# Gather depth, order of diagonals and evictions, and place of a residual in a PEER layer behind two transformer blocks

## The chip, the cores and the metric

The kernel runs on one core of one Trainium2 chip. The metric is the device time of one execution in microseconds, the median of several runs. Engines are named as in the profile: PE is TensorE (PEld its weight loads), DVE is VectorE, ACT is ScalarE, POOL is GpSimd and SP is SyncE.

## The reference

256 tokens of width 1024 pass through a first block (two layers, each with two SwiGLU FFNs around an attention mixer) and a second block, which ends with a PEER layer. Only that last layer is touched here. In outline, for a block of 128 tokens `xb` (normalized), with 8 heads, 128 sub-keys and a top 16:

```
q = (xb @ w_q).reshape(128, 8, 2, 128)
scores = einsum('thpd,hpkd->thpk', q, sub_keys)
top_s, top_i = top_k(scores, 16)
cand = all 16*16 sums of the two halves' scores
best_s, best_pos = top_k(cand, 16)
expert = index of the best (one of 16384)
gate = softmax(best_s)
act = gelu(einsum('thkd,td->thk', u[expert], xb))
y = einsum('thk,thkd->td', gate * act, v[expert])
```

`x + y` is the output. Everything is float32. Each token reads 8 x 16 = 128 experts, and an expert is a row of `u` and a row of `v`, 1024 numbers each.

## The kernel before, in words

Everything ahead of the PEER layer is a stream of weight units: SP loads a unit into one of nine `raw` tiles, ACT and DVE split it into a high and a low part, and TensorE multiplies. The change doesn't touch that part.

The PEER layer has two interwoven halves.

**Units.** The query projection `pq` has 16 units n, each 128 columns of `w_q` (16 matmuls on plain weights, L2044; the first five units are split ones). ACT evicts the unit's result into `QP` (L929). Two units make a head: after units 1, 4, 6, 8, 10, 12, 14 and 15 (`scored(n)`) TensorE computes that head's scores (L2061), and ACT evicts them (L935). Before unit n starts, TensorE waits for the eviction of unit n-1 or of the scores before it, since units and scores share two PSUM banks. DVE chooses the experts of a head in six steps (`route`, L1426 to L1469), which gives 16 index columns for each block of tokens. `shares` subtracts the maximum on DVE (L1477), ACT takes the exp (L904), and `gates` on DVE divides (L1482 to L1486).

**Slots.** The 2 x 128 pairs (block of tokens, expert rank) are 256 slots g. For slot g:

- POOL gathers 128 rows of `u` and `v` side by side into a tile of 128 x 2048 (L622, 1 MB). It waits until gather g-`FLYING` has landed, and until the slot that used the tile before is done on TensorE (`s_y`), or, for a tile's first use, until its former content is.
- DVE multiplies the `u` half with the tokens and sums (L1509, "dot").
- ACT applies gelu (L912), scales by the gate (L916), and writes a diagonal matrix of the weights (L920), into one of four buffers, so it waits for slot g-4 on TensorE.
- TensorE multiplies the diagonal with the `v` half (L2023, two matmuls of 512 columns) and adds into two PSUM banks of the block (`YB`). The residual enters the same banks at first, by eight matmuls with the identity (`begin`, L2013).

There are 15 tiles. Ten are free when the first gathers go; `raw` tiles are added when the last unit that used them is done: one at gather 10 (units 7 and 8), one at gather 14 (unit 10), one at gather 22 (unit 12), one at gather 34 (unit 15), and with it `XF`, the last unit's input.

**The order.** The order on each engine is written out. On TensorE and ACT, units 9 to 15 are mixed with slots 0 to 27: behind unit n come slots 4(n-9) to 4(n-9)+3 (`mixed(n)`); then slots 28 to 255 follow alone. On ACT the eviction of unit n comes ahead of these four slots' diagonals. DVE does the choosing of later heads ahead of every second slot: the table `CHOOSING` gives step number i of the list `later` to slot 2i, where twelve `route` steps, `shares` and `gates` of a pair of heads make 14 entries. ACT does the exp of `shares` ahead of the same slot in its own order. The first pair of heads is outside the table: its exp comes on ACT behind unit 8. The first residual, `begin(0)`, stands behind unit 8 on TensorE; the second, `begin(1)`, whose banks the units use until unit 15, behind slot 27.

```
for n in range(16):
    ac.wait_ge(*queried(n))
    ...
    if n == 8:
        shares(0, 0, 2)
    for g in mixed(n):
        slot(g)
```

Of the kernel before, what the change touches and what calls it, by code (L numbers as in the profile page):

```python
# [234 lines left out]
SLOTS = 15  # L235
QN_RING = 6
MIX0, MIX = 9, 4
FLYING = 4
ARENA = 17024


# [15 lines left out]
def program(nc, wst, cst, x, skt, uv, out, vscr, units):  # L257
    ctx = ExitStack()
    with ctx:
# [3 lines left out]
        def sem(name):  # L263
            return ctx.enter_context(nc.semaphore(name))
# [34 lines left out]
        def c(name, lo=0, hi=None):  # L299
            a0, a1 = at[name]  # L300
            return C[:, a0 + lo:(a1 if hi is None else a0 + hi)]

        def f32(ap):
            return ap.bitcast(F32)

        def flat(ap):
            return ap.rearrange("p a b -> p (a b)")
# [122 lines left out]
        s_txf, s_xtt, s_qp, s_scm, s_scr = (sem(n) for n in ("x_gained", "x_turned", "pq_out", "pq_scores",  # L430
                                                                 "scores_out"))
# [14 lines left out]
        def U(name, n):  # L446

            return split[where[name][n]] + 1
# [29 lines left out]
        def queried(n):  # L478

            if where["pq"][n] in split:  # L480
                return s_used, U("pq", n)
            return s_plain, plain_n[where["pq"][n]]
# [4 lines left out]
        def scored(n):  # L487
            return (0,) if n == 1 else (n // 2 - 1,) if n % 2 == 0 and n >= 4 else (7,) if n == 15 else ()

        def mixed(n):  # L490
            return range(MIX * (n - MIX0), MIX * (n - MIX0 + 1)) if n >= MIX0 else ()
# [10 lines left out]
        for k in sorted(range(4), key=lambda k: max(last[2 * k], last[2 * k + 1])):  # L502
            n = max(last[2 * k], last[2 * k + 1])
# [5 lines left out]
        for g in range(256):  # L509
            n = min((n for n in range(SLOTS) if rows[n][2] <= g), key=lambda n: taken[n][-1] if taken[n] else -1)  # L510
# [12 lines left out]
        CHOOSING, GATES = {}, {(0, 0): 1}  # L523
# [5 lines left out]
                    later += [("route", blk, hh, k) for hh in (h, h + 1) for k in range(6)]  # L529
                    later += [("shares", blk, h, 2), ("gates", blk, h, 2)]  # L530
        for n, what in enumerate(later):
            CHOOSING[2 * n] = (what,)

        def three(pe, o, wh, wl, xh, xl, start, stop):
            pe.matmul(o, wh, xh, start=start, stop=False, skip_group_check=True)  # L535
# [34 lines left out]
        def pool_program(po):  # L570
# [40 lines left out]
            for g in range(256):  # L611
                blk, s = g // 128, g % 128
                row, free, _ = rows[home[g]]
                if s % 16 == 0:
                    po.wait_ge(s_exi, g // 16 + 1)
                if g >= FLYING:
                    po.wait_ge(s_g[home[g - FLYING]], 16 * turn_of[g - FLYING])
                if before[g] is None:
# [7 lines left out]
        def act_program(ac):  # L626
# [3 lines left out]
            def hi(name, n):  # L630

                while at_m[0] < min(U(name, n) + AHEAD - 1, NSPL):
                    m = at_m[0]
                    i = spl_unit[m]
                    w = units[i][1]
                    ac.wait_ge(s_raw[i % RAW], 16 * (i // RAW + 1))
                    if m >= SPL:
                        ac.wait_ge(s_used, m - SPL + 1)
                    ac.activation(WH[:, m % SPL, 0:w], raw[:, i % RAW, 0:w], ACT.Copy).then_inc(s_hi, 1)  # L639
                    at_m[0] = m + 1  # L640
# [27 lines left out]
            def root(p):  # L668
                ac.wait_ge(s_sums, p + 1)
                ac.activation(RT[:, 0, :], PS[:, 7, 0:T], ACT.Sqrt, bias=c("eps", 0, 1), scale=1.0 / D).then_inc(s_rt, 1)  # L670
# [76 lines left out]
            for t in range(2):  # L747
                hi("uk", t)
                ac.wait_ge(s_pad, 1)
                for e in range(4):  # L750
                    n = 4 * t + e
# [93 lines left out]
            n = 4  # L845
# [54 lines left out]
            def shares(blk, h0, n):  # L900

                ac.wait_ge(s_bd, GATES[blk, h0])
                bd = BD[:, h0:h0 + n, :]
                ac.activation(bd, bd, ACT.Exp, scale=RTK[:, blk:blk + 1]).then_inc(s_bde, 1)  # L904

            def slot(g):
                blk, s = g // 128, g % 128
                for what in CHOOSING.get(g, ()):
                    if what[0] == "shares":
                        shares(*what[1:])  # L910
                ac.wait_ge(s_dot, g + 1)
                own(ac.activation(AG[:, blk, s:s + 1], AV[:, blk, s:s + 1], ACT.Gelu, scale=RTK[:, blk:blk + 1]))  # L912
                own.wait()
                if s % 32 == 0:
                    ac.wait_ge(s_gate, g // 32 + 1)
                own(ac.activation(WV[:, blk, s:s + 1], AG[:, blk, s:s + 1], ACT.Copy, scale=GA[:, blk, s:s + 1]))  # L916
                own.wait()
                if g >= 4:
                    ac.wait_ge(s_y, g - 3)
                ac.activation(DG[:, g % 4, :], c("ident"), ACT.Copy, scale=WV[:, blk, s:s + 1]).then_inc(s_dg, 1)  # L920
                if g == 127:
                    ac.wait_ge(s_y, 128)
                    ac.activation(OT[0], flat(PS[:, YB[0]:YB[0] + 2, :]), ACT.Copy).then_inc(s_ot, 1)

            for n in range(16):
                ac.wait_ge(*queried(n))
                if n >= QN_RING:
                    ac.wait_ge(s_scm, (n - QN_RING) // 2 + 1)
                ac.activation(QP[:, n % QN_RING, :], PS[:, bank_q[n], 0:T], ACT.Copy).then_inc(s_qp, 1)  # L929
                if n == 0:  # L930
                    hi("pq", 1)
                for h in scored(n):
                    ac.wait_ge(s_scm, h + 1)
                    for blk in range(2):
                        ac.activation(flat(SC[blk][:, 2 * h:2 * h + 2, :]), PS[:, bank_s[h], 256 * blk:256 * blk + 256],  # L935
                                      ACT.Copy).then_inc(s_scr, 1)
                if n == 1:
                    for kc in range(8):
                        ins = ac.activation(XF[:, kc, :], hT[:, kc, :], ACT.Copy, scale=c("gains", 64 + kc, 65 + kc))
                    ins.then_inc(s_txf, 1)  # L940
                    root(7)
                if n == 8:
                    shares(0, 0, 2)
                for g in mixed(n):
                    slot(g)

            for g in range(MIXED, 256):
# [569 lines left out]
        def pe_program(pe):  # L1517
# [195 lines left out]
            for n in range(8):  # L1713
                kv, g = n // 4, n % 4
# [37 lines left out]
            for r in range(4):  # L1752
                for t in range(2):
                    g = 2 * t + r % 2
# [26 lines left out]
            for e in range(2):  # L1781
                for blk in range(2):
                    for j in range(8):
                        g = 2 * (j // 4) + e
# [225 lines left out]
            def begin(blk):  # L2010

                for kc in range(8):
                    pe.matmul(PS[:, YB[blk] + kc // 4, 128 * (kc % 4):128 * (kc % 4) + 128],  # L2013
                              hT[:, kc, 128 * blk:128 * blk + 128], c("ident"), start=kc % 4 == 0, stop=False,
                              skip_group_check=True)

            def slot(g):
                blk, s = g // 128, g % 128
                pe.wait_ge(s_g[home[g]], 16 * turn_of[g])
                pe.wait_ge(s_dg, g + 1)  # L2020
                v = f32(rows[home[g]][0][:, 1024:2048])
                for q in range(2):
                    ins = pe.matmul(PS[:, YB[blk] + q, :], DG[:, g % 4, :], v[:, 512 * q:512 * q + 512], start=False,  # L2023
                                    stop=s == 127, skip_group_check=True)
                    if g == 255 and q == 0:
                        ins.then_inc(s_left, 1)
                ins.then_inc(s_y, 1)

            for n in range(16):
# [42 lines left out]
                    begin(0)  # L2072
                for g in mixed(n):
                    slot(g)
            pe.wait_ge(s_scr, 16)
            begin(1)
            for g in range(MIXED, 256):
                slot(g)

        block = ctx.enter_context(nc.Block())  # L2080
# [9 lines left out]
        @block.scalar  # L2090
        def _(eng):
            act_program(eng)
# [5 lines left out]
        @block.tensor  # L2098
        def _(eng):
            pe_program(eng)  # L2100
# [29 lines left out]
```

## Time and profile before

| | |
|---|---|
| median of 3 runs | 2061.48 us (2056.69 to 2062.80) |
| the profiled execution, its own time | 2058.03 us |
| its span | 2056.2 us |
| mean granted clock of TensorE | 0.969 |
| busy: PE, DVE, ACT, POOL | 1861.9, 1302.4, 907.1, 305.5 us |
| moved by DMA | 488.36 MB, of it 274.74 MB on the queue of POOL's gathers |

The span is what the profiler covers; the execution's own time is a little longer. Rows of the timelines stand in microseconds from the span's start. The PEER layer's first gather is issued at 1379.13 us, and the last dot begins at 2048.60 us. A busy share above 1 for the DMA engines means that packets overlap.

### The profile page before, as it was taken

Reading aid. Unit: us, or ns where it says so; the run is one execution under the profiler, and the core shown is the slowest. Engines: PE = TensorE matmul, PEld = TensorE weight load, DVE = VectorE, ACT = ScalarE, POOL = GpSimd, SP = SyncE. Lnnn points to the kernel's source line nnn. Section 1 sums busy time; section 2 is a strip of 40 time slices with the busy share of each in tenths; the row PEclk is TensorE's granted clock in tenths of the full one; section 3 lists DMA queues with packets and bytes.
Section 4 is the critical chain, followed back from the end, with each engine's and each line's share of the span. In section 5 each row is a group of like instructions: output and inputs, shape, how many; then the busy total and the mean of one; then the engine's idle time right before and its main releaser. Section 6 shows DMA issues by size and latency. Waiting matters only on the chain.

```text
span 2056.2 us, 29871 instructions
## 1 busy us (share of the span) xinstructions
PE 1861.9 (91%) x11568; PEld 1494.0 (73%) x11568; DVE 1302.4 (63%) x2378; ACT 907.1 (44%) x1865; POOL 305.5 (15%) x340
## 2 busy tenths in 40 slices
PE   7999999999999999999999988898897887777777
PEld 7999889999999999769999878786442332222222
DVE  5555885555655562786556766578297777776444
ACT  4444464444444431474444443543354444444333
POOL 1000101000100010000000000122333333333332
PEclk9999999999999997999999899999999999999999
DMA  7555426955455534205555233359899999999998
GB/s 272 185 185 177 132 72 145 315 186 185 154 185 185 185 123 145 82 27 171 184 187 182 87 129 103 114 184 367 316 418 421 421 421 418 419 420 417 414 422 346
DMA packets 96973, 488.36 MB, mean 238 GB/s; under 512 B 10640, under 2 KB 10896, under 8 KB 63808
## 3 DMA queue, kind: packets, MB, share of 16 engines
q0 software_dynamic: 38368, 274.74, 34.8%
q1 hardware_dynamic: 58464, 211.70, 30.2%
q8 instruction: 93, 1.52, 0.3%
q14 instruction: 48, 0.39, 0.1%
HBM read 482.21 MB, written 4.19 MB: 237 GB/s over the span
## 4 chain that ended last, share of the span: by engine, by line
PE 64%; issue 10%; DVE 10%; DMA 8%; POOL 5%; ACT 4%; POOLq 0%; ACTq 0%; SPq 0%; DVEq 0%
PE PS L535 16%; PE PS L537 15%; PE PS L536 15%; PE PS L2023 6%; DMA raw<-uv,A 2%; PE PS L2044 2%; DVE WL L967 2%; PE PS L1538 1%; DMA XL<-uv,A 1%; POOL raw L622 1%; DVE XL L975 1%; DMA A<-uv,A 1%; DMA XF<-uv,A 1%; DVE A L1267 1%; POOL WH L622 1%
## 5 line engine op out<-in xcount | busy, mean ns | idle before, releaser
L967 DVE TENSOR_TENSOR WL<-raw,WH 128x1024 fp32r<-128x1024 f32 (+1 forms) x379 | 451.6, 1233 | 92.3 <-ACT WH L639 91.7
L535 PE MATMUL PS<-XH,WH 128*128 128x256 f32 x1632 | 473.5, 290 | 30.0 <-DVE WL L967 16.0
L536 PE MATMUL PS<-XL,WH 128*128 128x256 f32 x1632 | 465.7, 285 | 0.0
L537 PE MATMUL PS<-XH,WL 128*128 128x256 f32 x1632 | 465.6, 285 | 0.0
L639 ACT ACTIVATE WH<-raw 128x1024 fp32r<-128x1024 f32 (+1 forms) x379 | 375.0, 1040 | 65.5 <-PE PS L537 34.2
L535 PEld LDWEIGHTS PS<-XH,WH 128*128 128x128 f32 x1632 | 315.0, 193 | 39.0 <-issue 19.4
L536 PEld LDWEIGHTS PS<-XL,WH 128*128 128x128 f32 x1632 | 315.6, 193 | 0.2
L537 PEld LDWEIGHTS PS<-XH,WL 128*128 128x128 f32 x1632 | 315.1, 193 | 0.0
L912 ACT ACTIVATE A<-A,RTK 128x1 f32<-128x1 f32 x256 | 74.9, 293 | 289.9 <-DVE A L1509 288.4
L535 PE MATMUL PS<-GH,WH 128*128 128x256 f32 x704 | 198.1, 281 | 0.0
L536 PE MATMUL PS<-GL,WH 128*128 128x256 f32 x704 | 197.8, 281 | 0.0
L537 PE MATMUL PS<-GH,WL 128*128 128x256 f32 x704 | 197.8, 281 | 0.0
L680 ACT ACTIVATE A<-A 128x256 f32<-128x256 f32 x88 | 36.7, 417 | 351.0 <-DVE A L996 351.0
L580 POOL TENSOR_TENSOR A<-hT 128x256 f32<-128x256 f32 x64 | 47.0, 756 | 953.1 <-DVE hT L1011 726.1
L535 PE MATMUL PS<-YH,WH 128*128 128x256 f32 x584 | 166.3, 285 | 5.2 <-DVE A L1115 3.1
L536 PE MATMUL PS<-YL,WH 128*128 128x256 f32 x584 | 165.1, 283 | 0.0
L537 PE MATMUL PS<-YH,WL 128*128 128x256 f32 x584 | 165.0, 283 | 0.0
L2023 PE MATMUL PS<-raw,A 128*128 128x512 f32 x260 | 127.7, 617 | 31.5 <-ACT A L920 31.5
L996 DVE TENSOR_TENSOR A<-PS,RT 128x512 f32<-128x512 f32 x88 | 60.8, 691 | 149.8 <-PE PS L537 149.4
L535 PEld LDWEIGHTS PS<-GH,WH 128*128 128x128 f32 x704 | 132.7, 188 | 0.1
L537 PEld LDWEIGHTS PS<-GH,WL 128*128 128x128 f32 x704 | 132.7, 188 | 0.0
L536 PEld LDWEIGHTS PS<-GL,WH 128*128 128x128 f32 x704 | 132.7, 188 | 0.0
(305 smaller groups left out, 3128.2 us busy)
## 6 DMA issues: line engine op xcount, KB each, us to landing
raw<-wst SPq DMA_DIRECT2D x388, 512.0 KB, 4.5
raw<-wst SPq DMA_DIRECT2D x9, 384.0 KB, 3.6
vscr<-A POOLq DMA_DIRECT2D x1, 3072.0 KB, 36.0
A<-vscr POOLq DMA_DIRECT2D x1, 2048.0 KB, 21.9
C<-cst SPq DMA_DIRECT2D x1, 1236.5 KB, 11.0
raw<-uv,A POOLq DMA_INDIRECT x65, 9.7
hT<-xin SPq DMA_DIRECT2D x2, 512.0 KB, 5.3
A<-vscr POOLq DMA_DIRECT2D x1, 1024.0 KB, 11.8
```

What stands on the lines that cost most here:

```text
L535: pe.matmul(o, wh, xh, start=start, stop=False, skip_group_check=True)
L536: pe.matmul(o, wh, xl, start=False, stop=False, skip_group_check=True)
L537: return pe.matmul(o, wl, xh, start=False, stop=stop, skip_group_check=True)
L580: po.tensor_tensor(SQ[:, kc, :], hT[:, kc, :], hT[:, kc, :], ALU.mult).then_inc(s_sq, 1)
L622: po.indirect_dma_start(row, None, uv if row.dtype == F32 else uv.bitcast(F32R), bass.IndirectOffsetOnAxis(ap=EX[:, blk, s:s + 1].bitcast( ...
L639: ac.activation(WH[:, m % SPL, 0:w], raw[:, i % RAW, 0:w], ACT.Copy).then_inc(s_hi, 1)
L680: ac.activation(GS[:, b, 0, :], GS[:, b, 0, :], ACT.Silu).then_inc(s_silu, 1)
L912: own(ac.activation(AG[:, blk, s:s + 1], AV[:, blk, s:s + 1], ACT.Gelu, scale=RTK[:, blk:blk + 1]))
L967: dv.tensor_tensor(WL[:, m % SPL, 0:w], raw[:, i % RAW, 0:w], f32(WH[:, m % SPL, 0:w]), ALU.subtract).then_inc(s_lo, 1)
L996: dv.tensor_tensor(GS[:, b], PS[:, b, :].rearrange("p (a t) -> p a t", a=2), RT[:, 1:2, :].broadcast_to([128, 2, T]), ALU.mult).then_inc(s ...
L2023: ins = pe.matmul(PS[:, YB[blk] + q, :], DG[:, g % 4, :], v[:, 512 * q:512 * q + 512], start=False, stop=s == 127, skip_group_check=True)
L2044: ins = pe.matmul(PS[:, bank_q[n], 0:T], R[:, 128 * kc:128 * kc + 128], XF[:, kc, :], start=kc == 0, stop=kc == 7, skip_group_check=True)
```

## The change

It has five edits. POOL lets up to eight gathers fly (`FLYING` 4 to 8). ACT makes the diagonals of the first two slots of `mixed(n)` ahead of the eviction of unit n, and the other two behind it. The exp of the first pair of heads stands behind unit 6 on ACT. The table `CHOOSING` starts at slot 2, so each of its steps comes two slots later, on DVE and for the exps on ACT. TensorE adds the second residual ahead of slot 64. Lines behind L925 are numbered two higher in the changed kernel, and those of TensorE's slots, too.

```diff
--- before.py
+++ after.py
@@ -235,7 +235,7 @@
 SLOTS = 15
 QN_RING = 6
 MIX0, MIX = 9, 4
-FLYING = 4
+FLYING = 8
 ARENA = 17024
 
 
@@ -529,7 +529,7 @@
                     later += [("route", blk, hh, k) for hh in (h, h + 1) for k in range(6)]
                     later += [("shares", blk, h, 2), ("gates", blk, h, 2)]
         for n, what in enumerate(later):
-            CHOOSING[2 * n] = (what,)
+            CHOOSING[2 * n + 2] = (what,)
 
         def three(pe, o, wh, wl, xh, xl, start, stop):
             pe.matmul(o, wh, xh, start=start, stop=False, skip_group_check=True)
@@ -923,6 +923,8 @@
                     ac.activation(OT[0], flat(PS[:, YB[0]:YB[0] + 2, :]), ACT.Copy).then_inc(s_ot, 1)
 
             for n in range(16):
+                for g in mixed(n)[:2]:
+                    slot(g)
                 ac.wait_ge(*queried(n))
                 if n >= QN_RING:
                     ac.wait_ge(s_scm, (n - QN_RING) // 2 + 1)
@@ -939,9 +941,9 @@
                         ins = ac.activation(XF[:, kc, :], hT[:, kc, :], ACT.Copy, scale=c("gains", 64 + kc, 65 + kc))
                     ins.then_inc(s_txf, 1)
                     root(7)
-                if n == 8:
+                if n == 6:
                     shares(0, 0, 2)
-                for g in mixed(n):
+                for g in mixed(n)[2:]:
                     slot(g)
 
             for g in range(MIXED, 256):
@@ -2072,9 +2074,10 @@
                     begin(0)
                 for g in mixed(n):
                     slot(g)
-            pe.wait_ge(s_scr, 16)
-            begin(1)
             for g in range(MIXED, 256):
+                if g == 64:
+                    pe.wait_ge(s_scr, 16)
+                    begin(1)
                 slot(g)
 
         block = ctx.enter_context(nc.Block())
```

On ACT, around unit 10 (L929, L931 in the changed kernel, evicts the unit; L935 or L937 its scores; L912, L916 and L920 are one slot), the order was:

```order
L929 ACTIVATE A<-PS 128x256
L935 ACTIVATE A<-PS 128x256 x2
L912 ACTIVATE A<-A,RTK 128x1
L916 ACTIVATE A<-A 128x1
L920 ACTIVATE A<-C,A 128x128
L912 ACTIVATE A<-A,RTK 128x1
L916 ACTIVATE A<-A 128x1
L920 ACTIVATE A<-C,A 128x128
```

and is now:

```order
L912 ACTIVATE A<-A,RTK 128x1
L916 ACTIVATE A<-A 128x1
L920 ACTIVATE A<-C,A 128x128
L912 ACTIVATE A<-A,RTK 128x1
L916 ACTIVATE A<-A 128x1
L920 ACTIVATE A<-C,A 128x128
L931 ACTIVATE A<-PS 128x256
L937 ACTIVATE A<-PS 128x256 x2
```

Slots 4 and 5 have moved from behind the two evictions to ahead of them.

On ACT, from unit 5 to unit 9, with the exp of the first pair of heads (L904) and the loads of the tables for exp and gelu, the order was:

```order
L929 ACTIVATE A<-PS 128x256 x2
L935 ACTIVATE A<-PS 128x256 x2
L929 ACTIVATE A<-PS 128x256 x2
L935 ACTIVATE A<-PS 128x256 x2
L904 ACT_TABLE_LOAD
L904 ACTIVATE A<-A,RTK 128x32
L929 ACTIVATE A<-PS 128x256
L912 ACT_TABLE_LOAD
```

and is now:

```order
L931 ACTIVATE A<-PS 128x256 x2
L937 ACTIVATE A<-PS 128x256 x2
L904 ACT_TABLE_LOAD
L904 ACTIVATE A<-A,RTK 128x32
L931 ACTIVATE A<-PS 128x256 x2
L937 ACTIVATE A<-PS 128x256 x2
L912 ACT_TABLE_LOAD
L912 ACTIVATE A<-A,RTK 128x1
```

The exp has moved ahead of the evictions of units 7 and 8; the gelu table's load now stands right behind unit 8's scores, where unit 9's eviction stood before it.

On ACT, around unit 15, with the exp of the second pair of heads (L904), the order was:

```order
L929 ACTIVATE A<-PS 128x256
L935 ACTIVATE A<-PS 128x256 x2
L904 ACT_TABLE_LOAD
L904 ACTIVATE A<-A,RTK 128x32
L912 ACT_TABLE_LOAD
L912 ACTIVATE A<-A,RTK 128x1
L916 ACTIVATE A<-A 128x1
L920 ACTIVATE A<-C,A 128x128
```

and is now:

```order
L912 ACTIVATE A<-A,RTK 128x1
L916 ACTIVATE A<-A 128x1
L920 ACTIVATE A<-C,A 128x128
L912 ACTIVATE A<-A,RTK 128x1
L916 ACTIVATE A<-A 128x1
L920 ACTIVATE A<-C,A 128x128
L931 ACTIVATE A<-PS 128x256
L937 ACTIVATE A<-PS 128x256 x2
L904 ACT_TABLE_LOAD
L904 ACTIVATE A<-A,RTK 128x32
L912 ACT_TABLE_LOAD
L912 ACTIVATE A<-A,RTK 128x1
```

Slots 24 and 25 stand ahead of the last eviction, and the second exp still stands between that eviction and the next diagonal, which is now slot 26's.

## Rows read from the trace of the kernel before

**Rows 1.** The page, part 2: GB/s in 40 equal slices of 51.4 us
```profile
GB/s 272 185 185 177 132 72 145 315 186 185 154 185 185 185 123 145 82 27 171 184 187 182 87 129 103 114 184 367 316 418 421 421 421 418 419 420 417 414 422 346
```

**Rows 2.** Windows: stretch, its us, busy us of each engine (x instructions), PEclk, DMA share, GB/s
```profile
1380.00:1408.00 28.00, 25.23 (x148) 22.52 (x146) 14.87 (x62) 8.13 (x19) 9.59 (x11) 0.99 1.02 395
1408.00:1500.00 92.00, 78.16 (x238) 44.74 (x239) 52.50 (x139) 34.95 (x109) 28.32 (x30) 0.93 0.88 330
1500.00:2040.00 540.00, 432.18 (x910) 160.74 (x909) 364.01 (x879) 235.03 (x680) 202.17 (x215) 0.98 1.05 420
```

**Rows 3.** Waits, 1404 to 1503 us: who waited <- for whom: sum, times, longest
```profile
ACT A L929 <- PE PS L2044: 52.7, 7, 10.2
...
POOL raw L622 <- PE PS L2044: 17.9, 3, 7.7
```

**Rows 4.** Timeline of POOL: start, us, instruction [idle before <- releaser]
```profile
1412.67 0.94 POOL L622 DMA_INDIRECT XH<-uv,A  x1 [7.87 <-PE PS L2023]
...
1439.13 1.10 POOL L622 DMA_INDIRECT WL<-uv,A  x1 [5.98 <-PE PS L2023]
...
1486.28 0.94 POOL L622 DMA_INDIRECT raw<-uv,A  x1 [7.69 <-PE PS L2044]
...
1500.94 0.94 POOL L622 DMA_INDIRECT A<-uv,A  x1 [1.58 <-DMA raw<-uv,A]
...
2038.91 0.94 POOL L622 DMA_INDIRECT YL<-uv,A  x1 [1.54 <-DMA A<-uv,A]
```

**Rows 5.** Timeline of TensorE, 1400 to 1505 us
```profile
1408.16 3.75 PE L2023 MATMUL PS<-XH,A 128*128 128x512 f32 x4 [2.93 <-ACT A L920]
...
1446.81 1.05 PE L2061 MATMUL PS<-A 128*128 128x128 f32 x8
1449.64 1.96 PE L2023 MATMUL PS<-XL,A 128*128 128x512 f32 x4 [1.78 <-ACT A L920]
...
1491.97 3.75 PE L2023 MATMUL PS<-XH,A 128*128 128x512 f32 x4 [4.84 <-ACT A L920]
...
1500.92 1.95 PE L2013 MATMUL PS<-C,hT 128*128 128x128 f32 x16
```

**Rows 6.** Timeline of ACT, 1398 to 1495 us
```profile
1401.99 0.32 ACT L904 ACTIVATE A<-A,RTK 128x32 f32<-128x32 f32 x1
...
1405.67 1.28 ACT L912 ACT_TABLE_LOAD   x1
...
1485.53 0.38 ACT L929 ACTIVATE A<-PS 128x256 f32<-128x256 f32 x1 [7.90 <-PE PS L2044]
1487.17 0.66 ACT L935 ACTIVATE A<-PS 128x256 f32<-128x256 f32 x2 [1.25 <-PE PS L2061]
...
1491.42 0.40 ACT L920 ACTIVATE A<-C,A 128x128 f32<-128x128 f32 x1
```

**Rows 7.** Timeline of DVE, 1390 to 1492 us
```profile
1394.00 0.18 DVE L1477 TENSOR_TENSOR A<-A 128x32 f32<-128x32 f32 x1
...
1445.84 1.22 DVE L1509 CUSTOM_DVE_ANT_0 WL<-WL,PS 128x1024 fp32r<-128x1024 f32 x1 [1.54 <-DMA WL<-uv,A]
...
1461.76 1.22 DVE L1509 CUSTOM_DVE_ANT_0 XL<-XL,PS 128x1024 fp32r<-128x1024 f32 x1 [1.26 <-DMA XL<-uv,A]
...
1489.49 0.19 DVE L1482 TENSOR_REDUCE A<-A 128x2 f32<-128x32 f32 x1 [26.50 <-ACT A L904]
```

**Rows 8.** The chain that ended last, merged: start, us, what
```profile
1443.52 3.45 PE PS L2044 x16
...
1502.87 37.78 PE PS L2023 x88
```

**Rows 9.** Windows of 4 and 5 us, the same columns
```profile
1400.00:1404.00 4.00, 4.00 (x28) 3.72 (x28) 1.55 (x9) 2.26 (x4) 1.07 (x2) 1.00 1.07 430
1408.00:1412.00 4.00, 3.84 (x5) 1.80 (x6) 3.90 (x12) 2.88 (x10) 0.00 (x0) 0.50 0.92 375
15.00:20.00 5.00, 5.00 (x33) 5.00 (x32) 3.78 (x4) 2.34 (x2) 0.00 (x0) 1.00 1.03 410
```

## The prediction

> **What bounds the kernel now.** I read the page's slices first: the last quarter moves 420 GB/s in slice after slice, while the first slices of the PEER part reach 316 to 418 [rows 1]. The windows put numbers on it. From 1500 to 2040 us the core moves 420 GB/s with DMA engines booked over 100%; from 1408 to 1500 it moves only 330; before that 395 [rows 2]. Each of the 256 gathers is 128 rows x 2048 x 4 bytes, 1.049 MB, and at 420 GB/s takes 2.50 us. So the tail is bound by the DMA engines, and time can be won in two ways only: by keeping them busy between 1408 and 1500, or by making them faster. The first stretch moved 92 x 330 = 30.4 MB, worth 72.3 us at 420, so **19.7 us are lost there, and that is the ceiling** of anything that only reorders work (some 1.7 us more in the 28 us at 395).
>
> Who loses them: the waits of 1404 to 1503 show POOL held 17.9 us by TensorE's weight units (L2044), and ACT 52.7 us at its eviction (L929), waiting for the same units [rows 3]. POOL's timeline shows it at single gathers: 11 leaves at 1412.67 after 7.87 us of waiting for a slot, 34 at 1486.28 after 7.69 us for a unit, 41 at 1500.94; from there to gather 255 at 2038.91 it is 214 gathers at 2.514 us [rows 4]. TensorE and ACT take turns: ACT evicts unit n, only then makes the diagonals of its four slots, and TensorE idles meanwhile: 2.93 us before slot 0, 1.78 us in a middle unit, 4.84 us before slot 24 [rows 5]. ACT's rows show what stands in that last gap: the eviction at 1485.53, the scores at 1487.17, and slot 24's diagonal only at 1491.42 [rows 6]. In between stand two table loads and the exp of the second gates, for which DVE waited 26.50 us, to 1489.49 [rows 7].
>
> **The parts of the change.**
>
> *Two diagonals ahead of each eviction.* Needed for it are dots 4k and 4k+1 (k = 0 to 6) before unit 9+k ends. DVE had dot 25 done at 1463.0, 22 us before unit 15's eviction [rows 6, 7], so the input is there. ACT then makes both diagonals while TensorE is in the slots and the unit before, and TensorE finds them when its unit ends. Its chain from the end of unit 9 (1408.16 - 2.93 = 1405.2 [rows 5]) to slot 28 becomes: 28 slots at 37.78/22 = 1.72 us, 48.1; six units at 3.45, 20.7; four score groups at 1.05 less their overlap with the next matmul, 0.9, in sum 3.6 [rows 5, 8]; the wait of unit 15's scores for its own eviction, 0.6. Unit 15 still has an exp between its eviction and slot 26. From that eviction's start to the end of the first diagonal behind the exp ACT took 1485.53 to 1491.82, 6.3 us [rows 6]; TensorE covers it with scores and slots 24 and 25, 5 us, which leaves a stall of 1.3. The sum is 74.3: slot 28 starts at 1479.5. Before, that point was 1502.87 [rows 8]. **TensorE's chain becomes 23.4 us shorter**, of which idle time is 14.8 (2.93, five gaps of about 1.66, 4.84, less the 1.3), the second residual 1.8, and most of the rest slow stretches: the granted clock was 0.50 at 1408 to 1412 [rows 9], the 1.2 GHz level, after 2.93 us of idling, and slot 0's matmuls took 3.75 us where slot 12's took 1.96, behind a gap of 1.78 us only [rows 5].
>
> *What the gathers make of it.* Gather g takes the tile that slot g-11 used (11 to 13), later g-12 (15 to 21), g-13 (23 to 33) and g-15; gathers 14, 22 and 34 wait for units 10, 12 and 15 instead. With an idle pipe a gather needs 1445.84 - 1439.13 = 6.7 us from its issue on POOL to the start of its dot [rows 4, 7], and two are at least 2.50 apart. Gather 10 is through at about 1413 (the engines run to nearly 1412 [rows 9]). By the chain above slots 0 to 3 end at 1407.0, 1408.7, 1410.4 and 1412.1, and slots 4, 8, 12, 16, 20 and 24 at 1418.2, 1428.6, 1439.8, 1450.1, 1461.3 and 1473.1, each with its three followers 1.72 apart. With 0.85 us from a slot's end to POOL's issue (0.76 from 1411.91 to 1412.67 [rows 4, 5]), every gather from 11 to 41 is in time but three: 14 lands 0.2 late, 22 lands 1.6 late (unit 12 ends at 1437.2, issue 1438.0, landing 1444.7), 34 lands 2.8 late (unit 15 ends at 1469.9, landing 1477.4). So gather 41 lands at 1413 + 31 x 2.49 + 4.6 = 1494.8 (2.49 here, for the 421 GB/s of most slices [rows 1]). Before, it was issued at 1500.94 upon gather 37's landing, and landed four intervals later, at 1510.4. **Gain 15.6 us.** The two sums agree: of 19.7 us lost, 4.6 stay.
>
> *The first exp behind unit 6.* DVE hands over its shares at 1394.0 [rows 7] and ACT answered at 1401.99 [rows 6]; now it answers at about 1395. It moves unit 7's eviction by 0.3 us at most, under unit 8's matmuls, and it lets dots 0 and 1 begin 6 us earlier, which the diagonals of slots 0 and 1 need to be ready at 1405. Also the load of the gelu table (1.28 us at 1405.67 [rows 6]) now lies ahead of unit 9's end. No term of its own; without it slots 0 and 1 would keep their 2.9 us.
>
> *Choosing two slots later.* DVE's work is the same. The second gates' exp moves to ACT's slot 26 and DVE waits for it at slot 28. It resumes at about 1474, at 1489.49 before, and then does a slot in 1.7 us (364.01 us busy for 215 slots [rows 2]), nearer 1.9 while it chooses, so slot 28's dot is done by 1476 and DVE is behind the landings until about slot 50. No gather waits for that: gather 43 needs slot 28 (1481) and would be due at 1500. Cost nothing; were DVE 10 us later, it would be the next bound.
>
> *Second residual at slot 64.* Eight matmuls, 1.95 us at 1500.92 [rows 5], go from the catching-up stretch to one in which TensorE is 80% busy (432 of 540 [rows 2]). Counted above, worth nothing more.
>
> *Eight gathers in flight.* In my chain the old rule, g waits for g-4, binds nowhere, since four in flight cover the 6.7 us at 2.5 each. In steady state the engines are full with four. So zero; at the start at most 0.3 us. Bounds: the fastest 4 us with four in flight moved 430 GB/s [rows 9], 2.44 us a gather instead of 2.514, which over 214 would be 16 us more; on the other side, at 15 to 20 us many 512 KB weight loads stand queued and the core moved 410 [rows 9], 2.56 us a gather, 10 us lost. I take the value of the row that is this very stream, 420. Of the page "DMA: Bandwidth & Descriptors" (the Trainium skill, section "Where 436 GB/s comes from"): it says that loads from HBM are bound at about 358 GB/s. By that rate the stretch from 1408 would have lost only 92 - 84.8 = 7 us and the change could bring some 3; the time would be about 2058. The trace disagrees with its 420 over 540 us, and so this gets no chance.
>
> **Sum.** 15.6 us off the profiled execution's 2058.03 gives 2042.4; its span was 2056.2. The median of the three runs is 3.4 above that execution, and I put the forecast on the median: 2061.5 - 15.6 = **2045.9 us**.
>
> **Rivals.**
> 1. *The depth makes the DMA faster.* For it: the mean interval is 2.514 us where most slices give 2.49, so there are hitches that a deeper queue might bridge. Against: the booked share is 1.05 over the whole stretch [rows 2]. It would give up to 16 us more, about 2030. The same page (the Trainium skill, "DMA: Bandwidth & Descriptors", section "Specifications") names 435 GB/s as the ceiling, which would be 2.41 us a gather. 9%.
> 2. *The supply of rows stays the bound.* ACT's wait for a dot now stands before an eviction, so a late gather delays a unit and all gathers behind it, or DVE's wait for the second exp takes over the bound. For it: DVE waited 26.50 us on ACT, and POOL issues in order. Against: dots are 15 us early in my chain. A gain of 3 to 8 us then, 2053 to 2058. 13% (5% of it within 0.3%).
> 3. *Slower: eight in flight cost bandwidth.* Descriptors of eight gathers mix at the engines and the interval grows. The gain of 15.6 over 214 gathers is used up at 2.514 + 0.073 = 2.587 us, 405 GB/s. At the 395 GB/s of 1380 to 1408, where gathers began beside weight loads [rows 2], it is 2.655 us, 30 us lost, net 14.6 slower: 2076. Against: nothing on the way gets more work. 7%.
> 4. *The change does nothing*, if the real limit of 1408 to 1500 is the tiles: 2061 or so. Against: gathers 11, 20 and 34 left upon TensorE's releases. 3%.
>
> **How the numbers follow.** The forecast has 68%. Its own error is the latency of 6.7 us (1 us more or less moves the three late gathers by as much each, 3 us) and 3 us of spread between executions. The range takes rival 1's nearer half and rival 2's better half: 2036 to 2055. About 0.3%, 6 us, is what a measurement here can tell from no change: faster 85% (68, 9 and 8), same 8% (5 and 3), slower 7%.
>
> **What would show it.** Right: the window 1408 to 1500 at over 395 GB/s; TensorE's idle time before each unit's first slot gone and full clock at 1408 to 1412; slot 28 at about 1480; gather 41's landing near 1495; 2.51 us a gather after 1510; POOL's first eight issues 1.24 us apart. Wrong: an interval other than 2.49 to 2.53 in the steady stretch (rivals 1 and 3), or ACT standing on a dot while a finished unit waits (rival 2).

## The result, and the profile after

Six runs of the changed kernel have a median of 2046.5 us (2043.29 to 2048.21), six runs of the kernel before beside them 2059.76 us (2055.63 to 2062.80). The ratio is 0.9935, with a 95% interval of 0.9920 to 0.9950: **13.3 us faster**. The forecast was 2045.9 us, in a range of 2036 to 2055. The profiled execution took 2047.32 us, with a span of 2045.4.

The windows of the changed kernel, with the columns of [rows 2]:

```profile
1380.00:1408.00 28.00, 25.31 (x140) 22.27 (x139) 16.77 (x64) 7.80 (x19) 9.67 (x11) 0.94 1.01 395
1408.00:1412.00 4.00, 4.00 (x15) 2.59 (x14) 3.86 (x12) 2.57 (x9) 0.00 (x0) 1.00 0.94 379
1408.00:1500.00 92.00, 89.83 (x284) 51.01 (x283) 63.08 (x168) 41.54 (x128) 35.80 (x38) 1.00 0.98 382
1500.00:2030.00 530.00, 420.88 (x874) 154.48 (x872) 352.26 (x849) 229.36 (x661) 194.98 (x207) 0.98 1.05 421
```

The stretch of 1408 to 1500 moves 382 GB/s where it moved 330 [rows 2], TensorE is busy for 89.83 of 92 us, and its clock is at the 2.4 GHz level (1.00) at 1408 to 1412 where it was 0.50 [rows 9]. The steady stretch is as before, at 421 GB/s (420 before). By my count the 92 us now lose 92 x (420 - 382)/420 = 8.3 us instead of 19.7.

TensorE's timeline of the changed kernel (columns as in [rows 5]):

```profile
1406.28 3.62 PE L2046 MATMUL PS<-XF,raw 128*128 128x256 f32 x16
1409.73 1.88 PE L2025 MATMUL PS<-XH,A 128*128 128x512 f32 x4
...
1474.97 1.16 PE L2063 MATMUL PS<-A 128*128 128x128 f32 x8 [0.47 <-ACT A L931]
1475.96 1.88 PE L2025 MATMUL PS<-XH,A 128*128 128x512 f32 x4
1477.68 1.88 PE L2025 MATMUL PS<-XL,A 128*128 128x512 f32 x4
1480.97 1.95 PE L2025 MATMUL PS<-A 128*128 128x512 f32 x4 [1.41 <-issue]
...
1484.48 1.88 PE L2025 MATMUL PS<-A 128*128 128x512 f32 x4
```

Slot 0 starts with unit 9's end and at full speed (its four matmuls in 1.88 us, 3.75 before [rows 5]). The gaps in front of the slots are gone but for one: 1.41 us ahead of slot 26, at 1480.97. Slot 28 starts at 1484.48, which is 74.75 us after slot 0.

POOL's timeline (gathers 10, 11, 22, 34, 41 and 255; compare [rows 4]):

```profile
1404.54 0.94 POOL L622 DMA_INDIRECT raw<-uv,A  x1 [13.07 <-PE PS L2046]
1412.37 0.94 POOL L622 DMA_INDIRECT XH<-uv,A  x1 [6.89 <-PE PS L2025]
...
1442.53 0.94 POOL L622 DMA_INDIRECT raw<-uv,A  x1 [5.96 <-PE PS L2046]
...
1475.27 0.94 POOL L622 DMA_INDIRECT raw<-uv,A  x1 [7.68 <-PE PS L2046]
...
1484.01 0.94 POOL L622 DMA_INDIRECT A<-uv,A  x1 [0.30 <-issue]
...
2018.13 0.95 POOL L622 DMA_INDIRECT YL<-uv,A  x1 [1.54 <-DMA raw<-uv,A]
```

Gather 34 leaves at 1475.27, 11.0 us earlier than before, and from gather 60 on each takes 2.512 us (2.517 before). What is odd stands elsewhere. The waits from 1380 to 1400 us have two rows that the kernel before doesn't have, with a releaser that the profile can't name:

```profile
ACT A L931 <- remote: 9.2, 1, 9.2
DVE RTK L986 <- remote: 6.5, 1, 6.5
```

Here are the timelines of TensorE, ACT and DVE at that place:

```profile
1387.07 0.60 PE L1551 MATMUL PS<-C,RT 1*128 1x1 f32 x4
1387.60 3.72 PE L2046 MATMUL PS<-XF,raw 128*128 128x256 f32 x16
1394.01 1.16 PE L2063 MATMUL PS<-A 128*128 128x128 f32 x8 [2.69 <-ACT A L931]
1395.00 8.76 PE L2046 MATMUL PS<-XF,raw 128*128 128x256 f32 x32
```
```profile
1383.72 0.66 ACT L937 ACTIVATE A<-PS 128x256 f32<-128x256 f32 x2 [0.51 <-PE PS L2063]
1393.57 0.66 ACT L931 ACTIVATE A<-PS 128x256 f32<-128x256 f32 x2 [9.19 <-remote]
```
```profile
1393.63 0.16 DVE L986 COPY RTK<-PS 128x2 f32<-128x2 f32 x1 [6.51 <-remote]
```

By the records TensorE ends unit 5 at about 1387.1 and the small matmuls of L1551 at 1387.6. ACT evicts unit 5 only at 1393.57, DVE copies L1551's result only at 1393.63, and SP starts its last two weight loads, which wait for unit 5 too, at 1393.57. **Three engines get TensorE's release some 6 us late, all at once.** What follows comes late with it: TensorE stands 2.69 us ahead of the next scores. Then units 7 and 8, the 32 matmuls from 1395.00, take 8.76 us, and 7.07 where the release is on time. The window says why:

```profile
1396.00:1400.00 4.00, 4.00 (x14) 3.22 (x13) 3.66 (x14) 1.16 (x1) 0.00 (x0) 0.65 1.04 411
```

The granted clock is 0.65 on average there, partly at the 1.2 GHz level, behind the 2.69 us of idling, so the stall costs another 1.7 us. Unit 9 ends at 1409.7 where my chain had it at 1405.2.

To compare executions I use the time from gather 0's issue to the last dot's start, called **S** below. Where gather 0 is issued differs from trace to trace (1376.0 to 1384.6 us) for reasons that lie ahead of the PEER layer. S is 669.47 us before and 658.55 in the changed kernel, a gain of 10.9; 15.6 would have been 653.9. The windows of 1408 to 1500 are not shifted with gather 0, so their GB/s are comparable only roughly.

### The profile page after: what moved, and what is told of

Same layout as the page of the kernel before. It is cut to its first block, busy times and chain, and to the rows that moved or that the text cites. A ratio compares the mean times of both kernels' runs of the same rounds, so it can differ in the third digit from the quotient of the medians.

```text
span 2045.4 us, 29867 instructions
## 1 busy us (share of the span) xinstructions
PE 1863.1 (91%) x11568; PEld 1495.6 (73%) x11568; DVE 1303.7 (64%) x2378; ACT 907.0 (44%) x1865; POOL 305.9 (15%) x340
## 3 DMA queue, kind: packets, MB, share of 16 engines
q1 hardware_dynamic: 58464, 211.70, 30.9%
## 4 chain that ended last, share of the span: by engine, by line
PE 61%; DMA 12%; DVE 11%; issue 8%; POOL 4%; ACT 3%; another core or an unknown queue 0%; POOLq 0%; ACTq 0%; SPq 0%; DVEq 0%
PE PS L535 16%; PE PS L536 15%; PE PS L537 15%; PE PS L2025 3%; DMA WH<-uv,A 3%; DMA YL<-uv,A 3%; DMA YH<-uv,A 2%; DMA raw<-uv,A 2%; DVE WL L969 2%; PE PS L2046 2%; PE PS L1540 1%; DMA A<-uv,A 1%; DMA WL<-uv,A 1%; DVE XL L977 1%; DMA XF<-uv,A 1%
## 5 line engine op out<-in xcount | busy, mean ns | idle before, releaser
L535 PE MATMUL PS<-XH,WH 128*128 128x256 f32 x1632 | 474.1, 290 | 28.9 <-DVE WL L969 15.6
L912 ACT ACTIVATE A<-A,RTK 128x1 f32<-128x1 f32 x256 | 75.0, 293 | 297.8 <-DVE A L1511 296.2
```

## The experiments

Two theories on the 4.7 us of S that are missing: (A) the late release costs them, and it has to do with eight gathers in flight at the start; (B) the supply of rows holds by something else that I did not count, and the late release is harmless. Besides, each part of the change was to be priced by itself.

**Four in flight in the changed kernel.**
```diff
-FLYING = 8
+FLYING = 4
```


> The changed kernel with four gathers in flight instead of eight, all else kept. In the changed kernel's trace the evictions of unit 5 (ACT), the copy of RTK (DVE) and SP's last two weight loads, which all wait for TensorE, came at 1393.57 although TensorE's matmuls had ended at 1387, and unit 9 ended at 1409.7 instead of 1405.2. Theory A, the depth causes that late release: the release comes at 1387 again, unit 9 ends at 1405.2, slot 28 begins at 1479.5 to 1480, and the time is 3 to 5 us below the changed kernel's, some 2042 (ratio to before 0.9915). Theory B, the late release is a chance event or comes of the reordering: the stall is seen here too, or is gone from both, and the time is the changed kernel's, 2046.5 (0.9935). Theory C, the depth brought part of the gain: 2050 or more.

Measured: 2044.08 us, ratio 0.9932 [0.9916, 0.9948]; S 653.63. No engine waits for an unnamed releaser, DVE's copy follows 0.59 us behind TensorE. DVE's row, the window of 1408 to 1500, and POOL's gathers 34 and 41:

```profile
1389.21 0.16 DVE L986 COPY RTK<-PS 128x2 f32<-128x2 f32 x1 [0.59 <-PE PS L1551]
```
```profile
1408.00:1500.00 92.00, 90.12 (x282) 50.55 (x281) 63.04 (x163) 42.12 (x131) 34.01 (x36) 1.00 1.02 405
```
```profile
1472.14 0.94 POOL L622 DMA_INDIRECT raw<-uv,A  x1 [7.35 <-PE PS L2046]
...
1486.17 0.94 POOL L622 DMA_INDIRECT A<-uv,A  x1 [1.54 <-DMA raw<-uv,A]
```

S is 15.8 us better than before, where the forecast said 15.6, and the window of 1408 to 1500 reaches 405 GB/s. So all of the gain is there without the greater depth.

**Eight in flight in the kernel before.**
```diff
-FLYING = 4
+FLYING = 8
```


> The kernel before with eight gathers in flight and nothing else. Theory A: the late release at 1393.5 is seen, TensorE's units 6 to 9 come 4.5 us late, and since TensorE's chain limits the tiles up to 1500 us, the kernel is 2 to 5 us slower than before, 2062 to 2065. Theory B: no stall, 2059.8, the same within 1 us. Theory C, the depth gives bandwidth: 2050 to 2055.

Measured: 2057.17 us, ratio 0.9992 [0.9982, 1.0002]; S 668.71, 0.8 less than before; 339 GB/s at 1408 to 1500. No late release. Depth alone is worth nothing that can be told, and it doesn't bring the late release here, as theory A expected it would.

**The diagonals behind the eviction again, the rest of the change kept.**
```diff
             for n in range(16):
-                for g in mixed(n)[:2]:
-                    slot(g)
                 ac.wait_ge(*queried(n))
...
-                for g in mixed(n)[2:]:
+                for g in mixed(n):
                     slot(g)
```


> The changed kernel with each unit's eviction ahead of all four diagonals again. If the two diagonals ahead are what pays: the gaps of 1.5 to 1.8 us before each unit's first slot come back, seven of them some 12 us, slot 28 begins 10 to 12 us later than in the changed kernel, and most of the gain is gone: 2054 to 2058. If it was the earlier exp and the later residual that paid: 2046 to 2049.

Measured: 2059.63 us, ratio 1.0003 [0.9991, 1.0015]; S 668.65. That is above the 2054 to 2058 expected: all of the gain is gone, not most of it. There is no late release. TensorE's timeline has its gaps back:

```profile
1450.20 1.96 PE L2023 MATMUL PS<-XL,A 128*128 128x512 f32 x4 [1.78 <-ACT A L920]
...
1489.47 1.96 PE L2023 MATMUL PS<-XH,A 128*128 128x512 f32 x4 [1.78 <-ACT A L920]
...
1494.42 1.95 PE L2023 MATMUL PS<-A 128*128 128x512 f32 x4 [1.28 <-ACT A L920]
```

**Without the two diagonals ahead of each eviction there is next to no gain**; early exp, later choosing, late residual and depth together give 0.8 us of S without them. The same kernel was traced once more:

> A second look at the changed kernel with every eviction ahead of all four diagonals. With eight in flight this order showed no late release so far. If the release is late by the number in flight alone, it should appear here too, at 1387 to 1394; if it needs the new order on ACT, it should not, and the span from first gather to last dot is 668 to 669 us again.

One execution of 2054.21 us, S 668.66, no late release. So S repeats to 0.01 us in these two traces, whose gather 0 lies 5 us apart. Where the release is late it repeats less well: two traces of the change itself, below, are 2.0 us apart.

**Eight in flight, but not at the start.**
```diff
-                if g >= FLYING:
-                    po.wait_ge(s_g[home[g - FLYING]], 16 * turn_of[g - FLYING])
+                fl = 4 if g < 16 else FLYING
+                if g >= fl:
+                    po.wait_ge(s_g[home[g - fl]], 16 * turn_of[g - fl])
```


> The changed kernel with four in flight for gathers 0 to 15 and eight from 16 on. Theory A (the depth hurts only at the start, where gathers meet the last units and loads): no late release at 1393, the time is that of four in flight, some 2042. If depth costs or gives something in the steady stretch, this run differs from the one with four in flight throughout by more than 2 us.

Measured: 2042.65 us, ratio 0.9934 [0.9912, 0.9955]; S 654.05; 404 GB/s; no late release. Depth behind gather 16 costs nothing and gives nothing.

**The changed kernel once more**, unchanged:

> The changed kernel once more, unchanged. In its first trace TensorE's release of unit 5 reached ACT, DVE and SP 6.4 us late, at 1393.57; in the trace with the depth alone, and in that with the eviction first, both with eight in flight, it came in time. If the late release is a chance event of one execution, it is absent here, and from gather 0's issue to the last dot it takes 654 us (658.6 in the first trace, 669.5 before). If the changed order and the depth together bring it about, it is seen again at about 12 us behind gather 0's issue, with 658 to 659 us. Time 2044 to 2047 either way, since the late release is worth 4 to 5 us.

Measured: 2048.75 us, ratio 0.9939 [0.9925, 0.9954]; S 656.52. The late release is there again: DVE waits 6.27 us for its copy, and ACT's eviction of unit 5 comes at 1397.33. But S is 2.0 us less than in the first trace and below the 658 to 659 expected, and the time is above the 2044 to 2047. The difference in S lies in TensorE: this time it stands 1.06 and 0.45 us instead of 2.69, its clock stays at 1.00 behind that, and units 7 and 8 take 7.17 us instead of 8.76. Measured from gather 0's issue, unit 9 begins at 22.5 us where the release is on time, at 24.5 here and at 27.1 in the first trace. Take that lateness (2.0 and 4.6 us) off S, and 654.5 and 653.9 are left: as in the kernels with four and six in flight (653.6 and 654.5). So the missing part of the gain is what the late release cost.

**The first exp behind unit 8 again.**
```diff
-                if n == 6:
+                if n == 8:
                     shares(0, 0, 2)
```


> The changed kernel with the first pair's exp behind unit 8 again. If the prediction's step is right (the exp must be early, so that the diagonals of slots 0 and 1 are ready when unit 9 ends): the exp is at 1402, dot 0 ends at 1404.1, the diagonals of slots 0 and 1 end at about 1405.2 and 1406.3, and unit 9's eviction comes 1 us late; gather 0 to last dot 654 to 655.5, so the early exp is worth 0 to 1.5 us. If it is a large part of the gain: 657 or more.

Measured: 2048.21 us, ratio 0.9940 [0.9919, 0.9961]; S 657.43, between the two traces of the changed kernel, with a late release (a wait of 6.25 us). Slot 0's diagonal was ready at 1409.6, with unit 9's end at 1409.5, and slot 0 began at 1409.77. So the early exp is not what makes the release late. Unit 9 begins 24.5 us behind gather 0 here too, as in the second trace of the change, whose S is 0.9 us less; with the lateness taken off, S is 655.4 against 653.9 and 654.5. An estimate from these figures puts the early exp at 0.9 to 1.5 us. A run without the late release would be needed to confirm it.

**The second residual ahead of slot 28 again.**
```diff
-                if g == 64:
+                if g == MIXED:
```


> The changed kernel with the second residual ahead of slot 28 again. By the prediction TensorE's slots from 28 on come 1.8 us later and no gather waits for them: gather 0 to last dot 654, no difference. If the catching-up stretch limits: 655.5 or more.

Measured: 2044.5 us, ratio 0.9916 [0.9894, 0.9939]; S 656.76, with the late release (6.31 us). The eight matmuls take their 1.8 us at 1484.92. Unit 9 begins 25.2 us behind gather 0, so 2.8 us of S are the late release's; 654.0 are left, the same as without the step. The place of the residual is worth nothing.

**Six in flight in the changed kernel.**
```diff
-FLYING = 8
+FLYING = 6
```


> The changed kernel with six in flight. If the late release grows with the number of gathers issued back to back, it is shorter than 6.3 us, perhaps 3, and the span from first gather to last dot is about 656 us. If it is all or nothing, it is either 6.3 us (657 to 658.5 us) or none (653.6 us).

Measured: 2043.33 us, ratio 0.9931 [0.9910, 0.9952]; S 654.48; 402 GB/s; no late release (DVE waits 0.59 us). So with six it isn't shorter, it is absent, in this one trace.

**Tiles of `raw` taken later, four in flight.** The three late gathers of the forecast wait for units 10, 12 and 15. At that point another tile, whose slot is done, is free for them, so the units' tiles can be taken a little later: unit 10's by gather 15 instead of 14, unit 12's by gather 24 instead of 22, and unit 15's tile and `XF` by gathers 37 and 38 instead of 34 and 35.
```diff
-            rows.append((flat(raw[:, 2 * k:2 * k + 2, :]), queried(n), early + MIX * max(n - MIX0, 0)))
-        rows += [(flat(XF[:, :, :]), queried(15), early + MIX * (15 - MIX0))]
+            rows.append((flat(raw[:, 2 * k:2 * k + 2, :]), queried(n), early + MIX * max(n - MIX0, 0) + max(n - MIX0, 0) // 3 + (n > MIX0)))
+        rows += [(flat(XF[:, :, :]), queried(15), early + MIX * (15 - MIX0) + 4)]
```


> The changed kernel with four in flight, and the tiles that wait for units 10, 12 and 15 taken by gathers 15, 24 and 37 (38 for XF) instead of 14, 22 and 34, so that gathers 14, 22, 23 and 34 to 36 use tiles of slots that are already done. By the prediction's chain the three late landings (0.2, 1.6 and 2.8 us) are what is left of the lost time: they go, gather 0 to last dot falls from 653.6 to about 649, and the window 1408 to 1500 moves 418 GB/s or more. Rival: TensorE's slots then limit, and it stays at 652 or more.

Measured: 2041.27 us, ratio 0.9908 [0.9890, 0.9925]; S 650.75. The window and POOL's gathers 22, 34 and 41:

```profile
1408.00:1500.00 92.00, 90.12 (x281) 50.29 (x280) 62.89 (x163) 41.36 (x127) 34.49 (x37) 1.00 1.06 421
```
```profile
1431.58 0.94 POOL L622 DMA_INDIRECT raw<-uv,A  x1 [1.56 <-DMA WH<-uv,A]
...
1461.53 0.94 POOL L622 DMA_INDIRECT WL<-uv,A  x1 [1.06 <-DMA YL<-uv,A]
...
1478.97 0.94 POOL L622 DMA_INDIRECT A<-uv,A  x1 [1.56 <-DMA raw<-uv,A]
```

Gathers 22, 34 and 41 now wait for landings in flight, and for no unit. So do gathers 15, 24 and 37, which take the units' tiles now (at 1414.20, 1436.54 and 1469.00). The stretch that lost 19.7 us before moves 421 GB/s: nothing is lost in it any more.

**The same with eight in flight.**

> As the best run so far, but with eight in flight. Theory (a late release at the start belongs to eight in flight with the new order on ACT): DVE waits about 6 us for a release at 1387 to 1394, units 6 to 9 are 4 to 6 us late, and the span from first gather to last dot is 654 to 656 us instead of 650.8. Rival (the late release was chance, or belongs to the early tiles): no such wait, 650 to 652 us, median 2041.

Measured: 2040.83 us, ratio 0.9914 [0.9894, 0.9933]; S 650.72; 421 GB/s. And no late release, by DVE's timeline:

```profile
1387.72 0.16 DVE L986 COPY RTK<-PS 128x2 f32<-128x2 f32 x1 [0.59 <-PE PS L1551]
```

This is a miss for my reading of it. The instructions up to gather 14 are the changed kernel's, in its order and with its eight in flight, and only the choice of tiles behind them differs. So eight in flight with the new order does not always bring the late release. One thing besides the tiles differs, though. The three later traces with the late release (the change again, the exp behind unit 8, the residual at slot 28) come from one chip. The four traces with eight in flight from the start and the release on time come from two others: this one and the second with the eviction first from one of them, the first with the eviction first and the one with the depth alone from the other. For the first trace of the change the chip isn't on record. No kernel with eight in flight from the start had its release on time on the chip of those three, so the chip may be part of the cause; no run tests it.

**The better version, with the choosing at slot 0 again.** Tiles later, four in flight, and
```diff
-            CHOOSING[2 * n + 2] = (what,)
+            CHOOSING[2 * n] = (what,)
```


> The changed kernel with four in flight, the raw tiles of units 10, 12 and 15 first taken one to three gathers later (as in the best run so far), and CHOOSING starting at slot 0 again. Theory (engines full from the start on, 650.8 us from first gather to last dot): the second exp moves ahead of slot 24, the 1.4 us gap before slot 26 goes to slot 24, DVE has its gates some 5 us earlier, and since no gather waits for DVE or for slot 26 the span from first gather to last dot stays at 650 to 652 us, median 2040 to 2043. Rival (dots of slots 28 to 50 that come late do hold tiles): 1 to 3 us less, 648 to 650.

Measured: 2040.66 us, ratio 0.9912 [0.9895, 0.9930]; S 650.29; 421 GB/s. TensorE's rows:

```profile
1469.81 1.16 PE L2063 MATMUL PS<-A 128*128 128x128 f32 x8 [0.47 <-ACT A L931]
1470.81 1.88 PE L2025 MATMUL PS<-raw,A 128*128 128x512 f32 x4
1472.53 1.88 PE L2025 MATMUL PS<-XL,A 128*128 128x512 f32 x4
1474.24 3.60 PE L2025 MATMUL PS<-A 128*128 128x512 f32 x8
```

Slots 24 to 27 follow without a gap; not even slot 24 has one, since its exp and table loads lie under unit 15. It brings 0.5 us of S, within what the theory said: with the engines full, TensorE's 1.4 us are worth next to nothing.

All of S side by side, with DVE's wait for its copy:

| kernel | in flight | ratio to before | S, us | GB/s, 1408:1500 | DVE's wait at L984/L986 |
|---|---|---|---|---|---|
| before | 4 | | 669.47 | 330 | 0.59 |
| eight in flight in it | 8 | 0.9992 | 668.71 | 339 | 0.59 |
| change, eviction first (two traces) | 8 | 1.0003 | 668.65, 668.66 | 339, 336 | 0.59, 0.59 |
| **the change** (two traces) | 8 | 0.9935, 0.9939 | 658.55, 656.52 | 382, 392 | 6.51, 6.27 |
| with the exp behind unit 8 | 8 | 0.9940 | 657.43 | 390 | 6.25 |
| with the residual at slot 28 | 8 | 0.9916 | 656.76 | 391 | 6.31 |
| six in flight | 6 | 0.9931 | 654.48 | 402 | 0.59 |
| eight behind gather 16 | 4, 8 | 0.9934 | 654.05 | 404 | 0.59 |
| four in flight | 4 | 0.9932 | 653.63 | 405 | 0.59 |
| tiles later, eight | 8 | 0.9914 | 650.72 | 421 | 0.59 |
| tiles later, four | 4 | 0.9908 | 650.75 | 421 | 0.59 |
| and choosing at slot 0 | 4 | 0.9912 | 650.29 | 421 | 0.59 |

The medians alone don't part the change from its versions with four, six or a late eight: their intervals overlap, and the start of gather 0 moves each execution by more than the 4 us in question. S parts them, though it rests on one trace of each kernel, and on two of the change and of that with the eviction first.

## Why the prediction was right, and where it was not

**The bound and the ceiling: right.** The core's DMA engines bind at 420 GB/s, and 19.7 us were to be had. The kernels with tiles taken later win 669.47 - 650.75 = 18.7 us and 19.2, and move 421 GB/s at 1408 to 1500. The Trainium skill's rule that loads from HBM are bound at about 358 GB/s ("DMA: Bandwidth & Descriptors", section "Where 436 GB/s comes from"), which I gave no chance, fails in every trace. The Trainium skill has in "Perfetto Trace Analysis", section "Roofline", what does agree: a single active core can pull more than that share, up to its DMA engines' 435 GB/s or so.

**TensorE's chain: right to half a microsecond.** From unit 9's end to slot 28 the forecast had 74.3 us, the trace has 74.75. The stall ahead of slot 26 was to be 1.3 and is 1.41; the scores' wait for unit 15's eviction was to be 0.6 and is 0.47. The clock at slot 0 is back at 1.00.

**Three gathers late: right in kind, 1.7 us too dear.** Taking exactly their tiles later brought 2.9 us of S (653.63 to 650.75), where the three were priced at 4.6.

**15.6 us for the gathers: right where TensorE's release is on time** (15.8 with four in flight, 15.4 with a late eight, 15.0 with six), and too much for the changed kernel as it stands, by 4.7 us in the first trace and 2.7 in the second. The step that failed is the start of the chain: I took unit 9's end at 1405.2 from the kernel before. Its end came at 1409.7, 4.5 us late, by TensorE's stall of 2.69 us, the 1.7 us at a lower clock behind it, and small parts. I also said of the greater depth "at the start at most 0.3 us"; whether that failed depends on what makes the release late, which stays open. I also wrote that over 395 GB/s at 1408 to 1500 would show me right; it was 382 and 392 in the two traces of the change.

**Why the median came out all the same:** the forecast stood on 2061.5, and six runs of the kernel before gave 2059.76, 1.7 lower; the gain by medians was 13.3, 2.3 less than forecast. The two nearly cancel. That 2046.5 lies 0.6 from the forecast is partly luck.

**Parts costed at nothing.** Depth: from gather 60 on the interval stayed at 2.51 to 2.52 us in every kernel, which rules out rivals 1 and 3. Residual: nothing. Choosing two slots later: DVE got its second gates at 1478.5 in the changed kernel,

```profile
1478.49 0.19 DVE L1484 TENSOR_REDUCE A<-A 128x2 f32<-128x32 f32 x1 [14.45 <-ACT A L904]
```

where it was 1489.49 [rows 7], and turning the step back gave 0.5 us in the best version. Early exp: some 0.9 to 1.5 us, by the estimate above. The forecast said that slots 0 and 1 would keep their 2.9 us without it; with the exp behind unit 8 TensorE had a gap of only 0.3 us ahead of slot 0. Rival 2 did not come. ACT did wait for dots, 8.6 us in six places, but TensorE waited for a diagonal only once, for 0.3 us. ACT's largest wait is still the one for TensorE at its eviction, in the waits of 1404 to 1503,

```profile
ACT A L931 <- PE PS L2046: 40.4, 8, 6.2
...
POOL raw L622 <- PE PS L2046: 30.9, 4, 13.1
```

and POOL's 30.9 us, more than the 17.9 of [rows 3], hold 13.07 that come from issuing its first ten gathers in 11.4 us and then waiting for unit 8.

**Theory A or B.** B falls: where the release is on time, the whole 15.6 are there, and with the lateness of unit 9 taken off they are there in the changed kernel too. Of A half stands. The late release costs 2 to 5 us of S (656.5 to 658.6 against 653.6 to 654.5). That it belongs to eight in flight at the start is not shown: it came in four of four traces of the change and its two near relatives, and in none of four others with eight from the start, which ran on other chips than three of those four.

## What to carry to other kernels

Where two engines hand a shared buffer back and forth, do the work that needs no release ahead of the wait: two of four diagonals in front of the eviction closed TensorE's gaps ahead of the units' first slots, and without them all but 0.8 us of the gain was gone. When the stream is bound by DMA, count only landings: look for the requests that leave late (here three tiles taken one to three gathers too early), and leave alone stalls that no transfer waits for. And measure a change of a few microseconds between two events inside its own stage, since what lies ahead of it moved by 8 us from one execution to another.

## What the runs showed of the hardware

**A release 6 us late.** In four traces (the change twice, with the exp behind unit 8, with the residual at slot 28) DVE, ACT and SP got TensorE's releases of unit 5 and L1551 up to 6.5 us behind the end of the matmuls in the records, while POOL issued gathers every 1.25 us beside 1.05 MB transfers. DVE's copy was 5.7 to 5.9 us later than the 0.59 us of the other traces each time. TensorE's own records show it going on to unit 6 at once. Ends of matmuls are modelled, but ACT's row bears this out: in the changed kernel it evicted units 5 and 6 back to back from 1393.57, 0.66 us for both. Unit 6's matmuls take 3.45 us and L1551's 0.5, so TensorE had ended unit 5 by 1389.9 at the latest, and at least 3.7 us of the delay are the release's and not the matmuls'. It was absent in ten traces of nine other kernels, among them four with eight in flight from the start. What makes it is open: neither the depth nor the order on ACT brings it alone, it came with either place of the exp and of the residual, and the chip isn't ruled out. A version with the first gathers issued further apart wasn't tried.

**Four gathers of 1.05 MB are enough.** They fill the DMA engines at 421 GB/s, as well as eight do in the kernels with tiles taken later; from gather 60 on, a gather takes 2.51 to 2.52 us in all kernels, with four, six or eight in flight.
